# A one-hot moving operand 48 elements further into its buffer, and the table buffer behind it moved by 64

## The reference

```python
s1, s2 = halves of the query against 128 sub-keys each      # per token and head
v1, i1 = lax.top_k(s1, 16); v2, i2 = lax.top_k(s2, 16)
top_s, top_pos = lax.top_k(all sums v1 + v2, 16)            # 8 heads x 16 picks per token
gates = jax.nn.softmax(top_s, axis=-1)
hid = jax.nn.gelu(jnp.einsum('cd,ced->ce', x_c, u_table[idx_c]), approximate=False)
return jnp.einsum('ce,ced->cd', gates * hid, v_table[idx_c])
```

## Time and profile before

| what | value |
|---|---|
| three timed executions | 945.51, 945.83, 950.56 us |
| median | 945.83 us |
| the profiled execution, its own time | 949.53 us |
| its span, first to last instruction | 947.8 us |
| TensorE matmuls | 6220 |
| matmuls of 256 columns in `hidden` | 3072 |
| matmuls of 256 columns in `gates` | 256 |

### The profile page before, as it was taken

The page is one execution under the profiler, slowest core; times in us unless marked ns, Lnnn a source line. Parts: engine busy times, 40 slices in busy tenths (PEclk is TensorE's granted clock), DMA queues, the critical chain, the costliest instruction groups (busy, mean ns, idle before and its releaser), DMA issues.

```text
span 947.8 us, 19175 instructions
## 1 busy us (share of the span) xinstructions
PE 940.5 (99%) x6220; PEld 858.1 (91%) x6220; DVE 688.2 (73%) x1389; ACT 615.4 (65%) x1039; POOL 333.8 (35%) x148
## 2 busy tenths in 40 slices
PE   9999999999999999999999999999999999999998
PEld 6988889999999999999999998888888888888887
DVE  6658864999987888888988865555555555566663
ACT  7678754556676888888888875445545445456643
POOL 0003500388887777777777781000000000000000
PEclk9999999999999999999999999999999999999999
DMA  9860453055555454544445455555567776555521
GB/s 341 320 241 1 174 208 124 24 183 192 179 187 179 168 177 158 176 162 170 160 172 170 162 178 189 190 198 193 186 240 242 230 256 224 189 188 199 185 103 45
DMA packets 46459, 172.08 MB, mean 182 GB/s; under 512 B 5043, under 2 KB 8668, under 8 KB 44892
## 3 DMA queue, kind: packets, MB, share of 16 engines
q1 hardware_dynamic: 46284, 171.53, 52.2%
q10 hardware_dynamic: 144, 0.15, 0.1%
HBM read 169.55 MB, written 2.11 MB: 181 GB/s over the span
## 4 chain that ended last, share of the span: by engine, by line
PE 91%; ACT 3%; DVE 2%; issue 2%; POOL 1%; DMA 0%; DVEq 0%; POOLq 0%; ACTq 0%
PE bank L1264 12%; PE bank L1265 12%; PE bank L1266 12%; PE pair L1600 12%; PE pair L1602 12%; PE pair L1603 12%; PE pair L1561 3%; PE pair L1299 1%; PE pair L1301 1%; PE pair L1300 1%; PE bank L1299 1%; PE bank L1301 1%; PE bank L1300 1%; PE bank L1645 1%; PE bank L1643 1%
## 5 line engine op out<-in xcount | busy, mean ns | idle before, releaser
L616 ACT ACTIVATE t_hi<-t_raw 128x1024 fp32r<-128x1024 f32 x256 | 270.3, 1056 | 166.7 <-DMA t_raw<-v_chunks 162.2
L1236 POOL TENSOR_TENSOR t_lo<-t_raw,t_hi 128x1024 fp32r<-128x1024 f32 x130 | 311.5, 2408 | 142.6 <-ACT t_hi L616 142.4
L1264 PE MATMUL bank<-xt_hi,t_hi 128*128 128x256 f32 x1024 | 286.5, 280 | 0.2 <-POOL t_lo L1236 0.2
L1265 PE MATMUL bank<-xt_lo,t_hi 128*128 128x256 f32 x1024 | 286.0, 279 | 0.0
L1266 PE MATMUL bank<-xt_hi,t_lo 128*128 128x256 f32 x1024 | 285.9, 279 | 0.0
L967 DVE TENSOR_TENSOR t_lo<-t_raw,t_hi 128x1024 fp32r<-128x1024 f32 x126 | 154.4, 1225 | 136.8 <-ACT t_hi L616 136.4
L1600 PE MATMUL pair<-t_hi,g_hi 128*128 128x512 f32 x512 | 199.5, 390 | 0.2 <-DVE g_lo L1147 0.2
L1602 PE MATMUL pair<-t_lo,g_hi 128*128 128x512 f32 x512 | 199.2, 389 | 0.0
L1603 PE MATMUL pair<-t_hi,g_lo 128*128 128x512 f32 x512 | 199.2, 389 | 0.0
L1264 PEld LDWEIGHTS bank<-xt_hi,t_hi 128*128 128x128 f32 x1024 | 193.5, 189 | 0.4 <-POOL t_lo L1236 0.4
L1266 PEld LDWEIGHTS bank<-xt_hi,t_lo 128*128 128x128 f32 x1024 | 193.6, 189 | 0.0
(11 more groups left out here) (285 smaller groups left out, 1283.6 us busy)
## 6 DMA issues: line engine op xcount, KB each, us to landing
t_raw<-u_chunks SPq DMA_DIRECT2D x128, 512.0 KB, 3.2
t_raw<-v_chunks SPq DMA_DIRECT2D x128, 512.0 KB, 3.3
w_raw<-w_query SPq DMA_DIRECT2D x4, 2048.0 KB, 7.9
w_raw<-w_in SPq DMA_DIRECT2D x3, 2048.0 KB, 10.5
w_raw<-w_out SPq DMA_DIRECT2D x2, 2048.0 KB, 8.2
wg_raw<-w_gate SPq DMA_DIRECT2D x8, 512.0 KB, 5.1
first_raw<-first SPq DMA_DIRECT2D x7, 384.0 KB, 6.1
w_raw<-w_in SPq DMA_DIRECT2D x4, 512.0 KB, 9.6
```

What stands on the lines that cost most here:

```text
L616: nc.scalar.activation(t_hi[:, q % RING, :], t_raw[:, q % RING, :], ACT.Copy).then_inc(t_hi_ready, 1)
L1236: nc.gpsimd.tensor_tensor(t_lo[:, q, :], t_raw[:, q, :], t_hi[:, q, :].bitcast(f32), ALU.subtract).then_inc(t_lo_pool, 1)
L1264: mm(dst, ah, bh, start=(c == 0), stop=False)
L1265: mm(dst, ah, bl, start=False, stop=False)
```

## The change

`hot_j` begins 48 elements later in its place. Its end would then run into `t_hi`, so `t_hi` begins 64 elements later, and with it every tile behind it in `ZONE` and `BIG` itself with all that lies there. No instruction is added, removed or reordered.

```diff
         ZONE = at
-        BIG = ZONE + 4 * 13312
+        BIG = ZONE + 4 * 13376
...
         hot_i = tile("hot_i", [P, 2, 4, P], ZONE + 4 * 4096, f32r)
-        hot_j = tile("hot_j", [P, 2, 4, 2, P], ZONE + 4 * 5120, f32r)
+        hot_j = tile("hot_j", [P, 2, 4, 2, P], ZONE + 4 * (5120 + HI_AT), f32r)
         g_hi = tile("g_hi", [P, RING, SEQ], ZONE + 4 * 4096, f32r)
         g_lo = tile("g_lo", [P, RING, SEQ], ZONE + 4 * 5120, f32r)
-        t_hi = tile("t_hi", [P, RING, D], ZONE + 4 * 7168, f32r)
-        o = ZONE + 4 * 11264
+        t_hi = tile("t_hi", [P, RING, D], ZONE + 4 * 7232, f32r)
+        o = ZONE + 4 * 11328
...
-        low = tile("low", [P, 2, 4, P], ZONE + 4 * 12032)
-        gate_hi = tile("gate_hi", [P, SEQ], ZONE + 4 * 12032, f32r)
-        gate_lo = tile("gate_lo", [P, SEQ], ZONE + 4 * 12288)
+        low = tile("low", [P, 2, 4, P], ZONE + 4 * 12096)
+        gate_hi = tile("gate_hi", [P, SEQ], ZONE + 4 * 12096, f32r)
+        gate_lo = tile("gate_lo", [P, SEQ], ZONE + 4 * 12352)
```

## The result

Over 22 executions each, the changed kernel took 949.44 us (median; 946.39 to 954.59) and the kernel before 946.6 (945.35 to 950.56). The ratio is 1.0029, with a 95% interval of 1.0018 to 1.0039. It is a small loss, where I had forecast a small gain. 949.44 lies just inside the range of 939.0 to 949.6, but by luck: that range was made for the forecast and for rival A, and what happened here had no chance in it. It lies well away from 943.3. The profiled execution of the changed kernel took 950.97 us.

A forecast was written before the change was run, and what follows sets the result against it. TensorE, 99% busy, was taken to be bound by how fast matmuls follow each other. Gates at 48 would save 6.25 us of the profiled 949.53, giving 943.28, likeliest 943.3 us; range of 8 in 10 runs 939.0 to 949.6.

The forecast's parts named there:

- rival A: Late steps: rate flips at gate sets go on; at most 0.7 us gained, 945 to 946 or 949 us; chance 0.25.
- Part (1): Late steps: `hot_j` at 48 matches `hidden`, so gate sets keep the fast rate; 257.04 us for the stage, gain 6.25 us.
- the two values given: Whole kernel, late steps fast: 943.3 us (chance 0.32) or 939.6 us (0.27), by the rate before the transposes.
- Part (2): `t_hi` and all behind it moved by 64 elements: claimed not to matter to matmul rates, costed at nothing.
- Part (3): Late steps: VectorE and ScalarE stay ahead of faster TensorE; tightest release, line 1116, keeps 0.33 us less some 0.11 us.
- rival B: Restart after the transposes at 284.94 us lands in the middle rate, which lasts: 950.6 or 954 us; chance 0.16.
- The two kinds of execution: Stretch from 188.73 to 284.94 us: fast near 945.7 us, middle in the profiled run and 950.56; worth 3.7 us.
- The rule on ports: TensorE's moving-operand reads: by the rule offset cannot change their rate, no gain, 945.8 us; trace said 120.0 against 113.3 ns.

The follow-up runs named there:

- `shift_only`: Changed kernel with `hot_j` back at offset 0, `t_hi` and all behind it still 64 elements further: 946.18 us, ratio 1.0002 to the kernel before.
- `one_buffer`: Changed kernel with only the first of the two `hot_j` buffers at offset 48, the second at a multiple of 64: 945.48 us in one execution.
- `late_order`: Changed kernel with `hidden`'s PSUM banks in the late steps alone reordered to 4, 6, 4, 5: 940.14 us, ratio 0.9939 to the kernel before.

## Why the prediction was wrong

**Part (1), the offset, was right.** Equal offsets keep the rate through a gate set (the chain up to 373.65, the set-by-set pattern with one buffer), and the stage all fast takes 257.04 us, as summed. The gain of 6.25 us exists: with the release out of the way the kernel takes 940.1 to 941.1 us, between the two values given, 939.6 and 943.3.

**Part (2), the move by 64, was right**: ratio 1.0002.

**Part (3), the cover, is the step that failed.** I put the margin of line 1116 at 0.33 us, took 0.11 off for the faster stream, and called it positive. It was mis-sized in each of its terms:
- The margin was counted up to the matmul at 349.81. What waits is the weight load ahead of it, which in the kernel before started at 349.70: release at 349.48, so 0.22 us and not 0.33.
- The load comes forward by 0.20 us and not by 0.11. I had counted 24 matmuls at the two rates. But the late steps go in rounds of four, three with a gate set and one without, and VectorE's work from the line 1116 of the first step to the releasing line 1116 of the fourth takes 11.85 us in both kernels (337.63 to 349.48, 361.96 to 373.81), and it starts 0.72 us behind a set. Only TensorE gets faster meanwhile. Its three intervals from the first set of a round to the set ahead of the load are 3.21 + 3.29 + 5.93 = 12.43 us in the earlier trace rows and 3.17 + 3.17 + 5.89 = 12.23 all fast; the starts of the sets give the same, 349.35 - 336.91 = 12.44 before and 373.49 - 361.25 = 12.24 after. So the sum could have been made from the earlier trace rows.
- A load starts some time behind the release that it waited for: 0.12 us at 373.93, 0.06 at 332.92. I had counted nothing.

The two ends of this stretch, before and after:

```profile
336.91 0.64 PE L1561 MATMUL pair<-hot_j,hot_i 128*128 128x256 f32 x4
...
337.63 0.42 DVE L1116 TENSOR_TENSOR slots<-slots,bank 128x256 f32 x1 [0.80 <-ACT bank L680]
```

```profile
361.25 0.62 PE L1561 MATMUL pair<-hot_j,hot_i 128*128 128x256 f32 x4
...
361.96 0.42 DVE L1116 TENSOR_TENSOR slots<-slots,bank 128x256 f32 x1 [0.47 <-ACT bank L680]
```

0.22 - 0.20 = 0.02 us, less than the 0.06 to 0.12 that the release needs to arrive. The prediction said what follows ("if it were gone, TensorE would wait there, and each wait may restart the stream at either rate") and gave it no chance and no price.

**The price follows from the two rates.** A fast stream ran into the wait four times in the 110 us of the two traces in which it was fast. In the first two rounds VectorE's work takes 11.6 us and there is room; from the third round on a fast stream met the wait in each round but one, the one that starts at 348.94 us, when an earlier wait had held TensorE back. Two of the four waits ended the fast rate. A middle stream has 0.5 us of room and never waited. So a fall is final: in both traces of the changed kernel the middle rate holds from the break to the end of the stage. Against the alternation, which was an even mixture, an early fall loses up to the 3.97 us of rival B, a late one would gain up to 6.25. In the two traces it came 73 and 37 us into a stage of 264, which made the stage 1.1 and 2.4 us longer than before. It is rival B's outcome by another road: not the restart at the transposes, but a wait inside the stage. For the other 21 of the 22 executions this is argued, as they left no trace. A fall where the second trace has it, with the slower stretch ahead of the transposes, would come to 950.97 + 1.25 = 952.2 us; three of the 22 lie above that, up to 954.59, and what they had is not shown.

**Rival B's own place was wrong for this offset, and right for another.** At 48 the stream left the transposes fast in all ten traces, whether it came in at the middle rate (before, after) or fast (the other eight, `shift_only`, `one_buffer` and `late_order` among them). At 16 it came in fast and left at the middle rate, and the stage took 267.11 us, where the prediction had priced 267.26.

**The two kinds of execution** came out as supposed: the stretch from 189 us to the transposes was at the middle rate in both profiled executions near 950 us, before and after, and fast, at 113.3 ns, in those of `shift_only` (946.22 us), `late_order` (939.16 us) and the changed kernel once more (948.12 us). What decides it at the wait at 188.73 was not tested.

**The rule on ports** of the Trainium skill (SBUF — State Buffer, section "SBUF: two separate sides"), that TensorE never waits for anyone, had been set against the earlier trace rows. The rule speaks of engines that wait for each other, and no run here shows TensorE in such a wait at a port. That a start address could therefore not matter was my own step from it, and that step fails: between 48, 32 and 16 only the addresses of the moving operands differ, and with them the time by up to 19 us.

## What to carry to other kernels

A faster stream needs its releases earlier, so before an engine with no idle time is made faster, take the margin of every release it depends on, from the end of the releasing instruction to the weight load (not the matmul). Take off how far the faster stream gets ahead over the whole stretch in which the releasing engine goes on at its own pace, and the time that a release takes to arrive. Where one engine's throughput depends on the pattern of its own stream, make the pattern the same in all its parts, then remove the waits inside it: the first alone lost 0.3% here, both together gained 0.6%. And read streams by distances of starts at fixed marks; busy shares and idle columns were the same in kernels 1% apart.

## What the runs showed of the hardware

- With a load of 128 columns for each matmul of 256, a stream of float32 matmuls settled at one rate, at a full granted clock (0.999 to 1.000). The rate depended on where the moving operand began, in elements modulo 64: 120.0 ns a matmul at 0, 113.3 or 117.8 at 16 and 48, 118.6 at 32, 117.3 or 118.7 at 40, 118.3 at 56. Where an offset had two, it also depended on how the stream was last interrupted. The fast rate then held for as long as 257 us, over loop ends and semaphore waits that were already satisfied. A move of the standing operand by 64 elements changed nothing (946.18 against 946.26 us).
- A late start by some 20 ns was once enough to change the rate for the rest of the stage (333.01 in the second trace of the changed kernel), and once not (337.11 in the first). What decides between the two was not found.
- Four matmuls at another offset changed the rate each time: 64 sets of 64 in the kernel before, every second one with one buffer moved.
- Matmuls of 512 columns, with a load of 128 columns each and both operands at multiples of 64 elements, were 226.7 ns apart in all traces and showed no second rate. Why the rates have the values that they have stays open.
